# Subtracting two softmaxes on TensorE, with a diagonal of ratios, while the weights are turned: one layer of a streaming encoder on one Trainium2 core

## The chip, the cores and the metric

The kernel runs on one core of a Trainium2 chip. The metric is the device time of one execution in microseconds. Before the change three runs gave 3885.79, 3887.19 and 3892.57 us, median 3887.19 us. The engines are TensorE (PE in the profile, its weight loads PEld), VectorE (DVE), ScalarE (ACT), GpSimd (POOL) and SyncE (SP), and 16 DMA engines move data.

## What is computed

A layer is applied to a prompt of 1024 rows and to 32 rows of a running stream that has 1024 past rows. Everything is float32. The part around the change is differential attention, 8 heads:

```python
s = jnp.einsum('bqhcd,bkhcd->bhcqk', q, k).astype(jnp.float32) * (HEAD_DIM ** -0.5)
visible = k_pos[None, :] < (q_pos[:, None] // CHUNK + 1) * CHUNK
s = jnp.where(visible, s, -jnp.inf)
p = jax.nn.softmax(s, axis=-1)
a = p[:, :, 0] - lam * p[:, :, 1]
return jnp.einsum('bhqk,bkhe->bqhe', a.astype(v.dtype), v)
# then, per head: o = rmsnorm(o, subln_g) * (1 - lam_init)
```

Beside it stand the projections (`z = xn @ w_in`), a short gated convolution, the merge of both branches with sigmoid gates and `w_o`, and a retrieval layer (PEER): each row scores 2 x 128 sub-keys in each of 8 heads, picks 16 of 16384 experts per head, and sums 128 expert rows weighted by a gate and a GELU of a dot product. The cast, norms and the caches are as usual.

## The kernel before

The 1056 rows are nine tiles: tiles 0 to 7 of 128 rows, tile 8 of the 32 stream rows. They are handled in three blocks of three tiles each (`BLOCKS`, L46): tiles 0-2, 3-5, 6-8. Each block has an attention part (`attend`) and then a part of dense products (`middle`). Since the experts of a tile are known only when its block's `middle` is over, the gather of experts of one block runs beside the attention and products of the next.

The backbone is a loop over 1056 slots `q`: one slot is one expert for each of a tile's 128 rows. GpSimd gathers 128 expert rows of 8 KB (L737) into one of nine ring buffers; VectorE forms the 128 dot products (`dot`, L1669); ScalarE applies GELU and the gate (L1256, L1260) and writes a diagonal of the weights (L1267); TensorE adds the weighted rows into PSUM with that diagonal (`weigh`, L1037). 226 of the 1056 slots are added by VectorE (L1680) in place of TensorE. A ring buffer is free for another gather when its row has been added.

Everything else is laid between slots by number: each engine's program yields "due at slot x", and `advance` issues it when the loop reaches that slot (`step_at`, with a pace of 0.93 or less slots per position and seven positions per tile and head, L50-L55). No engine reorders that list, so each runs its instructions in the written order and waits at semaphores.

For one head and one tile (a unit) `attend` does this: scores of both components (L791, mask L795) on TensorE, two row maxima on VectorE (L1477), two exponentials with their sums on ScalarE (L1101) into `pr[:, 0]` and `pr[:, 1]`, then `difference` on VectorE. With unnormalised weights e1, e2 and sums Z1, Z2 it forms `rl = -lambda * Z1 / Z2` (L1483, L1485, one number per row) and `pr0 = e1 + rl * e2` over all keys (L1488); the common factor 1/Z1 is taken up by the norm behind it. `turn_weights` then transposes `pr0` in blocks of 128 keys (L831) into PSUM bank 7, in two halves where there are more than four blocks; ScalarE copies them to SBUF (L1114), and `weigh_values` multiplies them with the values (L850). A unit of tile t has (t+1) key blocks: 4, 5, 6 in the second block of rows and 7, 8 in the third; tile 8 has 8 blocks of 128 keys and one of 32, all with 32 rows. So over 8 heads the second block turns 8 x 15 = 120 key blocks, the third 8 x 15 = 120 of full width and 72 of 32 rows. The exponentials of the next unit wait for `at_d`, that is until this unit's weights are turned.

In the rows below, names stand for buffers: `tl_ps` is PSUM, `tl_u` the scratch space that holds `pr`, `ident` the identity, `tl_dg` the diagonals of the slots, `ringx` and `mix` the ring buffers, `low` the weights' buffers and `tl_xr` normed rows or earlier keys and values.

Of the kernel before, what the change touches and what calls it, by code (L numbers as in the profile page):

```python
# [8 lines left out]
ALU = mybir.AluOpType  # L9
# [4 lines left out]
P = 128  # L14
# [52 lines left out]
def rows_of(t):  # L67

    return DEC if isinstance(t, int) and t == NT else P
# [14 lines left out]
def parts(tensor, first, n, width):  # L84

    return tensor[:, first:first + n * width].rearrange("p (n w) -> p n w", n=n)
# [164 lines left out]
def key_count(t):  # L251

    return (t + 1) * P if t < NT else PAST + DEC
# [7 lines left out]
def turned(w):  # L261

    return sum(turns(BLOCKS[x // 24][2][x % 3]) for x in range(w))


def half_of(b):

    return slice(b * P // 2, (b + 1) * P // 2)
# [23 lines left out]
def build_tail(nc, A, keep):  # L292

    with ExitStack() as ctx:
        def sb(name, shape, dt=F32):
            return ctx.enter_context(nc.sbuf_tensor("tl_" + name, shape, dt))
# [19 lines left out]
        pr = parts(u1, 0, 2, 1056)  # L316
# [16 lines left out]
        rope = sb("rope", [P, 3, 4, HD])  # L333
        ss4, rr4 = sb("ss4", [P, 2, 4]), sb("rr4", [P, 2, 4])
        nb, Z = sb("nb", [P, 2, 2]), sb("Z", [P, 2, 2])
        rl, zz = sb("rl", [P, 1]), sb("zz", [P, 2])
        so, ro = sb("so", [P, 2]), sb("ro", [P, 2])
        early, late = sb("early", [P, P]), sb("late", [P, CHUNK])
        xnr, cvT, oT = xr[:, 0], xr[:, 1], xr[:, 2]
# [48 lines left out]
        ident, ut = keep["ident"], keep["ut"]  # L388
# [363 lines left out]
        def _(pe):  # L752
# [16 lines left out]
            def attend(rb):  # L769
# [49 lines left out]
                def turn_weights(g, i, first, last_block):  # L819
                    t, w = tiles[i], 3 * g + i  # L820
                    n, nk = rows_of(t), key_count(tiles[i])
                    if first == 0:
                        pe.wait_ge(s["df_d"], w + 1)
                        if w:
                            pe.wait_ge(s["op_d"], w)
                    else:
                        pe.wait_ge(s["at_c"], turned(w) + 1)
                    for k in range(first, last_block):
                        m = min(P, nk - k * P)
                        o = ps[:m, 7, k * DEC:(k + 1) * DEC] if t == NT else ps[:, 7, k % 4 * P:(k % 4 + 1) * P]  # L830
                        last = nc.tensor.transpose(o, pr[:n, 0, k * P:k * P + m], ident[:n, :n])  # L831
                    last.then_inc(s["at_d"], 1)

                def weigh_values(g, i):
# [57 lines left out]
                for u in range(-3, 3 * DC + 1):  # L892
# [27 lines left out]
                    if here:  # L920
                        blocks = (key_count(t) + P - 1) // P
                        yield step_at(rb, h, base + TW)
                        turn_weights(g, i, 0, blocks if turns(t) == 1 else 4)
                        if turns(t) == 2:
                            yield step_at(rb, h, base + TW2)
                            turn_weights(g, i, 4, blocks)
# [138 lines left out]
            for b in range(2):  # L1065
                for h in range(2):
                    last = nc.tensor.matmul(ps[:DEC, 2 + h, :], sel[half_of(h), :], xb[half_of(h), 1, b * 512:(b + 1) * 512],
                                            start=b == 0, stop=b == 1)
# [245 lines left out]
        def _(dve):  # L1314
# [154 lines left out]
            def attend(rb):  # L1469
# [9 lines left out]
                def difference(g, i):  # L1479
                    t, w = tiles[i], 3 * g + i  # L1480
                    n, nk = rows_of(t), key_count(t)
                    dve.wait_ge(s["ex_d"], 2 * w + 2)
                    nc.vector.reciprocal(rl[:n, :], Z[:n, w % 2, 1:2])  # L1483
                    dve.drain()
                    nc.vector.scalar_tensor_tensor(out=rl[:n, :], in0=rl[:n, :], scalar=keep["neglam"][:n, 0:1],  # L1485
                                                   in1=Z[:n, w % 2, 0:1], op0=ALU.mult, op1=ALU.mult)
                    dve.drain()
                    nc.vector.scalar_tensor_tensor(out=pr[:n, 0, 0:nk], in0=pr[:n, 1, 0:nk], scalar=rl[:n, 0:1],  # L1488
                                                   in1=pr[:n, 0, 0:nk], op0=ALU.mult, op1=ALU.add).then_inc(s["df_d"], 1)

# [69 lines left out]
                for u in range(-3, 3 * DC + 1):  # L1560
# [12 lines left out]
                    if here:  # L1573
                        if t == NT:
                            yield step_at(rb, h, base + MX1)
                            row_max(g, i, (1,))
                        yield step_at(rb, h, base + (DF1 if t == NT else DF))
                        difference(g, i)
# [128 lines left out]
def build(nc, A):  # L1707
    with ExitStack() as ctx:
        def sb(name, shape, dt=F32):
            return ctx.enter_context(nc.sbuf_tensor(name, shape, dt))  # L1710

        keep = {"ut": sb("ut", [P, DC, 2]), "ident": sb("ident", [P, P]), "mhalf": sb("mhalf", [P, 8]),
                "mix": sb("mix", [P, DC * ROWS]), "ringx": sb("ringx", [P, (RING - 4) * 2 * D]), "low": sb("low", [P, WRING * D]),
                "subg": sb("subg", [P, VD]), "neglam": sb("neglam", [P, 1])}
        keep["xnT"] = parts(keep["mix"], 0, DC, 3 * P)
        keep["gain1"] = keep["mix"][:, DC * ROWS - 3 * D:DC * ROWS - 2 * D]
        keep["tab"] = keep["ringx"][:, 0:(NT + 1) * 4 * HD].rearrange("p (t k d) -> p t k d", k=4, d=HD)
        build_norm1(nc, A, keep)
        build_tail(nc, A, keep)
# [79 lines left out]
```

## Time and profile before

| | |
|---|---|
| median of three runs | 3887.19 us |
| profiled execution, device time | 3888.07 us |
| profiled execution, span | 3886.3 us |
| attention of the second block, about | 780 to 1190 us (24 units) |
| products of the second block | 1190 to 1750 us |
| attention of the third block, about | 1850 to 2385 us (24 units) |
| TensorE busy in the span | 82%, granted clock 0.875 |
| VectorE busy in the span | 65% |

The span is what lies between the first and last recorded instruction; the device time is 1.8 us more. Busy time of an engine in a stretch is the union of its recorded instructions, with a matmul's latency in it. A float32 matmul leaves two records, each with its weight load; a transpose leaves one. The granted clock is 1.00 at 2.4 GHz and 0.50 at 1.2 GHz; a mean between them tells how much of a stretch was spent at either.

### The profile page before, as it was taken

What the parts mean: (1) busy time and instruction counts of PE and PEld (TensorE: products, weight loads), DVE (VectorE), ACT (ScalarE), POOL (GpSimd) and SP (SyncE); (2) the same over time, 40 slices, a digit from 0 to 9 for tenths busy, and PEclk for the clock granted to TensorE, in tenths of its full rate; (3) what the DMA queues carried; (4) which work ended last, traced back from release to release, by engine and by line L of the source; (5) the groups of instructions that cost most, each with busy time, mean ns of one, the idle gap of its engine ahead of it and who ended that gap; (6) DMA issues with size and microseconds to landing.
All of it is one profiled execution on the core that took longest, in us unless ns stands there. A gap on an engine that the chain in (4) does not pass through costs nothing.

```text
span 3886.3 us, 46444 instructions
## 1 busy us (share of the span) xinstructions
PE 3170.0 (82%) x14521; PEld 1452.2 (37%) x14521; DVE 2520.5 (65%) x5855; ACT 1457.8 (38%) x4432; POOL 1498.6 (39%) x1410
## 2 busy tenths in 40 slices
PE   6999997888987999798788787878879667666666
PEld 3555554434443554353333333545335111111111
DVE  3333005988888964777777786886578754556664
ACT  2222002256754244222556565234333333333333
POOL 2111002355654432424455554434354433344442
PEclk9999998889998999898899998988889766666676
DMA  4322336799999999998899999999999999999998
GB/s 161 99 90 78 118 103 233 314 369 365 417 397 396 412 417 394 398 365 323 330 350 388 360 368 412 417 416 417 400 418 417 393 420 420 420 420 419 410 420 335
DMA packets 252964, 1340.70 MB, mean 345 GB/s; under 512 B 27344, under 2 KB 66032, under 8 KB 117296
## 3 DMA queue, kind: packets, MB, share of 16 engines
q0 software_dynamic: 152400, 1108.54, 70.5%
q1 hardware_dynamic: 95472, 215.95, 15.3%
q10 hardware_dynamic: 4848, 13.24, 0.9%
q8 instruction: 117, 1.92, 0.2%
q14 instruction: 127, 1.04, 0.1%
HBM read 1310.49 MB, written 27.15 MB: 344 GB/s over the span
## 4 chain that ended last, share of the span: by engine, by line
PE 46%; DMA 25%; DVE 14%; ACT 8%; issue 3%; DVEq 2%; POOL 1%; ACTq 1%; SPq 0%; POOLq 0%
DMA mix<-in_peer_uv,tl_idx 14%; PE tl_ps L1037 9%; PE tl_ps L983 9%; DMA ringx<-in_peer_uv,tl_idx 8%; PE tl_ps L816 7%; PE tl_ps L1020 4%; PE tl_ps L964 4%; PE tl_ps L996 3%; PE tl_ps L881 3%; DVE mix L1669 2%; PE tl_ps L791 2%; DVE ringx L1669 2%; PE tl_ps L850 2%; DMA mix<-in_peer_uv,tl_itop 1%; DVE tl_xa L1680 1%
## 5 line engine op out<-in xcount | busy, mean ns | idle before, releaser
L737 POOL DMA_INDIRECT ringx<-in_peer_uv,tl_idx x568 | 671.1, 1182 | 919.2 <-PE tl_ps L1037 624.2
L1669 DVE CUSTOM_DVE_ANT_0 ringx<-ringx,tl_xb 128x1024 f32<-128x1024 f32 x585 | 708.6, 1221 | 304.5 <-DMA ringx<-in_peer_uv,tl_idx 273.3
L1037 PE MATMUL tl_ps<-ringx,tl_dg 64*64 64x512 f32 x3808 | 649.5, 769 | 295.8 <-ACT tl_dg L1267 281.4
L737 POOL DMA_INDIRECT mix<-in_peer_uv,tl_idx x456 | 542.7, 1190 | 786.0 <-PE tl_ps L1037 460.7
L1256 ACT ACTIVATE tl_hg<-tl_hd 128x1 f32<-128x1 f32 x1056 | 213.3, 202 | 1436.5 <-DVE tl_hd L1669 1423.0
L1669 DVE CUSTOM_DVE_ANT_0 mix<-mix,tl_xb 128x1024 f32<-128x1024 f32 x471 | 571.5, 1221 | 244.0 <-DMA mix<-in_peer_uv,tl_idx 217.7
L1037 PE MATMUL tl_ps<-mix,tl_dg 64*64 64x512 f32 x2832 | 481.0, 761 | 225.2 <-ACT tl_dg L1267 223.4
L983 PE MATMUL tl_ps<-tl_xr,low 128*128 128x384 f32 (+1 forms) x1280 | 402.5, 471 | 5.0 <-DVE tl_xr L1627 5.0
L1037 PEld LDWEIGHTS tl_ps<-ringx,tl_dg 64*64 64x64 f32 x3808 | 120.6, 155 | 681.3 <-ACT tl_dg L1267 569.9
L1260 ACT ACTIVATE tl_hw<-tl_hg,tl_gw 128x1 f32<-128x1 f32 x1024 | 301.5, 294 | 72.8 <-issue 3.3
L983 PEld LDWEIGHTS tl_ps<-tl_xr,low 128*128 128x128 f32 x1280 | 248.0, 197 | 175.1 <-issue 44.1
L1267 ACT ACTIVATE tl_dg<-tl_eye,tl_hw 128x64 f32<-128x64 f32 x830 | 288.7, 348 | 59.8 <-issue 2.6
L816 PE MATMUL tl_ps<-low,tl_xr 128*128 128x384 f32 (+1 forms) x768 | 297.7, 535 | 15.7 <-DMA low<-in_watt 12.5
L1037 PEld LDWEIGHTS tl_ps<-mix,tl_dg 64*64 64x64 f32 x2832 | 86.9, 154 | 520.3 <-ACT tl_dg L1267 455.3
L1020 PE MATMUL tl_ps<-tl_xr,low 128*128 128x384 f32 (+1 forms) x768 | 263.7, 483 | 1.2 <-ACTq L1228 1.2
L964 PE MATMUL tl_ps<-tl_xr,low 128*128 128x384 f32 (+1 forms) x768 | 236.3, 466 | 0.6 <-ACT tl_xr L1127 0.6
L816 PEld LDWEIGHTS tl_ps<-low,tl_xr 128*128 128x128 f32 (+1 forms) x768 | 137.1, 189 | 191.5 <-issue 104.2
L1020 PEld LDWEIGHTS tl_ps<-tl_xr,low 128*128 128x128 f32 x768 | 140.3, 195 | 135.0 <-issue 75.5
L964 PEld LDWEIGHTS tl_ps<-tl_xr,low 128*128 128x128 f32 x768 | 149.3, 198 | 98.9 <-issue 31.9
L1477 DVE TENSOR_REDUCE tl_nb<-tl_ps 128x1 f32<-128x128 f32 (+5 forms) x144 | 110.6, 805 | 81.4 <-PE tl_ps L795 51.5
L1680 DVE SCALAR_TENSOR_TENSOR tl_xa<-mix,tl_hw,tl_xa 128x1024 f32<-128x1024 f32 x117 | 149.8, 1281 | 5.1 <-issue 4.7
L1634 DVE TENSOR_TENSOR tl_u<-tl_ps,tl_u 128x384 f32<-128x384 f32 (+1 forms) x48 | 25.0, 521 | 191.5 <-PE tl_ps L983 187.2
(205 smaller groups left out, 3878.5 us busy)
## 6 DMA issues: line engine op xcount, KB each, us to landing
low<-in_wall SPq DMA_DIRECT2D x240, 512.0 KB, 7.8
low<-in_watt SPq DMA_DIRECT2D x60, 512.0 KB, 8.3
ringx<-in_peer_uv,tl_idx POOLq DMA_INDIRECT x568, 14.9
mix<-in_peer_uv,tl_idx POOLq DMA_INDIRECT x456, 14.4
ringx<-in_watt SPq DMA_DIRECT2D x12, 512.0 KB, 6.8
tl_u<-in_x_prompt SPq DMA_DIRECT2D x8, 512.0 KB, 11.2
x_rows<-tl_u SPq DMA_DIRECT2D x8, 512.0 KB, 8.1
xs_rows<-tl_u SPq DMA_DIRECT2D x8, 512.0 KB, 8.1
```

Of the source, the lines that this page charges most:

```text
L737: nc.gpsimd.indirect_dma_start(out=ring[q % RING].rearrange("p a d -> p (a d)"), out_offset=None, in_=A["peer_uv"], in_offset=bass.Indirec ...
L816: last = nc.tensor.matmul(o, xn[:, c, i * P:i * P + n], w[:, :, c, :], start=(c == 0), stop=(c == DC - 1))
L881: last = nc.tensor.matmul(ps[:, (3, 5, 3)[k], 0:nr], w[:, c, :], xn[:, c, 0:nr], start=(c == 0), stop=(c == DC - 1))
L964: last = nc.tensor.matmul(ps[:, 2 + 3 * (cc % 2) + k, 0:n], w[:, c, :], xnr[:, c, 0:n], start=(c == 0), stop=(c == DC - 1))
L983: last = nc.tensor.matmul(ps[:, 2 + k, 0:n], w[:, c, :], src[k][:, c, 0:n], start=(c == 0), stop=(c == DC - 1))
L1020: last = nc.tensor.matmul(ps[:, 2 + qb % 2, 0:n], w[:, c, :], xT[:, c, 0:n], start=(c == 0), stop=(c == DC - 1))
L1037: last = nc.tensor.matmul(ps[half_of(h), b, :], dg[rows, npe(q) % DIAGS, :], ring[q % RING][rows, 1, h * 512:(h + 1) * 512], start=k == 0, ...
L1256: nc.scalar.activation(hg[:, j:j + 1], hd[:, j:j + 1], ACT.Gelu)
L1260: gate = nc.scalar.activation(hw[:, j:j + 1], hg[:, j:j + 1], ACT.Copy, scale=table(gw, tops, t)[:, k:k + 1])
L1267: nc.scalar.activation(dg[:, npe(q) % DIAGS, :], eye[:], ACT.Copy, scale=hw[:, j:j + 1]).then_inc(s["dg_done"], 1)
L1669: nc.vector.tensor_tensor_reduce(out=ring[q % RING][:, 0, :], in0=ring[q % RING][:, 0, :], in1=xb[:, t % 2, :], scale=1.0, scalar=0.0, op0 ...
L1680: nc.vector.scalar_tensor_tensor(out=xa[:], in0=ring[q % RING][:, 1, :], scalar=hw[:, k % TOPK:k % TOPK + 1], in1=xa[:], op0=ALU.mult, op1 ...
```

## The change

For the second and third block `difference` no longer touches the weights. VectorE multiplies the 128 x 128 identity by `rl` (one number per row) and so makes a diagonal matrix `ratio`. TensorE then makes each turned block as a sum of two matmuls in PSUM: e1-block times identity plus e2-block times `ratio`. In both, the weights that are loaded are the block of `pr`, and identity or ratio is what streams past. The first block keeps its subtraction and its transposes.

```diff
-        rl, zz = sb("rl", [P, 1]), sb("zz", [P, 2])
+        rl, zz, ratio = sb("rl", [P, 1]), sb("zz", [P, 2]), sb("ratio", [P, P])
...
                     for k in range(first, last_block):
                         m = min(P, nk - k * P)
                         o = ps[:m, 7, k * DEC:(k + 1) * DEC] if t == NT else ps[:, 7, k % 4 * P:(k % 4 + 1) * P]
-                        last = nc.tensor.transpose(o, pr[:n, 0, k * P:k * P + m], ident[:n, :n])
+                        if rb == 0:
+                            last = nc.tensor.transpose(o, pr[:n, 0, k * P:k * P + m], ident[:n, :n])
+                            continue
+                        nc.tensor.matmul(o, pr[:n, 0, k * P:k * P + m], ident[:n, :n], start=True, stop=False, skip_group_check=True)
+                        last = nc.tensor.matmul(o, pr[:n, 1, k * P:k * P + m], ratio[:n, :n], start=False, stop=True, skip_group_check=True)
                     last.then_inc(s["at_d"], 1)
...
                     dve.drain()
+                    if rb:
+                        nc.vector.tensor_scalar(ratio[:n, 0:n], ident[:n, 0:n], rl[:n, 0:1], None, ALU.mult).then_inc(s["df_d"], 1)
+                        return
                     nc.vector.scalar_tensor_tensor(out=pr[:n, 0, 0:nk], in0=pr[:n, 1, 0:nk], scalar=rl[:n, 0:1],
                                                    in1=pr[:n, 0, 0:nk], op0=ALU.mult, op1=ALU.add).then_inc(s["df_d"], 1)
```

Due slots, semaphores and their counts are unchanged. Below, TensorE's order at the first unit of the second block (tile 3, four key blocks), before:

```order
L816 MATMUL tl_ps<-low,tl_xr 128x384 x2
L1037 MATMUL tl_ps<-ringx,tl_dg 64x512 x4
L831 MATMUL tl_ps<-ident,tl_u 128x128 x4
L1037 MATMUL tl_ps<-mix,tl_dg 64x512 x4
L791 MATMUL tl_ps<-tl_xr,tl_u 128x384 x2
```

The same place with the change (line numbers behind L831 are higher by four, L1037 is L1041; `tl_ratio` is the diagonal of ratios):

```order
L816 MATMUL tl_ps<-low,tl_xr 128x384 x2
L1041 MATMUL tl_ps<-ringx,tl_dg 64x512 x4
L834 MATMUL tl_ps<-ident,tl_u 128x128
L835 MATMUL tl_ps<-tl_ratio,tl_u 128x128
L834 MATMUL tl_ps<-ident,tl_u 128x128
L835 MATMUL tl_ps<-tl_ratio,tl_u 128x128
L834 MATMUL tl_ps<-ident,tl_u 128x128
L835 MATMUL tl_ps<-tl_ratio,tl_u 128x128
L834 MATMUL tl_ps<-ident,tl_u 128x128
L835 MATMUL tl_ps<-tl_ratio,tl_u 128x128
L1041 MATMUL tl_ps<-mix,tl_dg 64x512 x4
L791 MATMUL tl_ps<-tl_xr,tl_u 128x384 x2
```

Nothing moved against its neighbours: four transposes became eight matmuls at the same place, ahead of a slot's weighted addition and of the next unit's scores. VectorE's order in a unit of tile 4 (L1669 is the dot product of a slot, L1507 the rotation of the next head's projection), before:

```order
L1483 RECIPROCAL tl_rl<-tl_Z 128x1
L1485 SCALAR_TENSOR_TENSOR tl_rl<-tl_rl,neglam,tl_Z 128x1
L1488 SCALAR_TENSOR_TENSOR tl_u<-tl_u,tl_rl 128x640
L1669 ISA ringx,tl_hd<-ringx,tl_xb 128x1024
L1669 ISA tl_hd 128x1
```

And with the change (seven lines further down in the file, from L1494 on):

```order
L1487 RECIPROCAL tl_rl<-tl_Z 128x1
L1489 SCALAR_TENSOR_TENSOR tl_rl<-tl_rl,neglam,tl_Z 128x1
L1493 TENSOR_SCALAR tl_ratio<-ident,tl_rl 128x128
L1676 ISA ringx,tl_hd<-ringx,tl_xb 128x1024
L1676 ISA tl_hd 128x1
```

One operation over 640 columns became one over 128, with the dot product of a slot queued right behind it as before.

## Rows read from the trace of the kernel before

**Rows 1.** The page: span, busy time by engine, slices of 97 us.

```profile
span 3886.3 us, 46444 instructions
PE 3170.0 (82%) x14521; PEld 1452.2 (37%) x14521; DVE 2520.5 (65%) x5855; ACT 1457.8 (38%) x4432; POOL 1498.6 (39%) x1410
PE   6999997888987999798788787878879667666666
PEclk9999998889998999898899998988889766666676
```

**Rows 2.** Windows by stage: busy us (x instructions), clock, DMA share, GB/s.

```profile
780.00:1190.00 410.00, 352.69 (x2013) 170.71 (x2015) 343.54 (x758) 253.92 (x745) 243.13 (x224) 0.94 0.97 388
1190.00:1750.00 560.00, 523.97 (x2029) 264.33 (x2026) 407.71 (x867) 187.85 (x523) 214.81 (x175) 0.96 0.99 396
1850.00:2385.00 535.00, 435.60 (x2410) 188.05 (x2410) 398.89 (x776) 310.88 (x847) 275.47 (x249) 0.91 0.94 364
3000.00:3886.00 886.00, 580.71 (x2872) 112.66 (x2868) 528.09 (x1127) 312.26 (x1065) 347.20 (x338) 0.68 0.99 407
```

**Rows 3.** Chain of waits, shares by line: second block, then third block.

```profile
by line: PE tl_ps L816 15.2%; PE tl_ps L1037 13.5%; DVE ringx L1669 5.1%; issue 4.7%; PE tl_ps L850 3.7%; DVE mix L1669 3.7%; ACT tl_u L1101 3.6%; ACT L1256 3.4%; PE tl_ps L791 3.4%; ACT L1101 2.8%; ACT tl_hw L1260 2.2%; DVE tl_oh L1388 2.0
by line: PE tl_ps L816 13.0%; PE tl_ps L1037 12.4%; PE tl_ps L791 10.7%; PE tl_ps L850 6.7%; ACT tl_u L1101 6.4%; DMA low<-in_watt 5.2%; issue 5.1%; ACT L1101 4.8%; ACT L1256 4.6%; ACT tl_hw L1260 3.1%; ACT tl_dg L1267 2.2%; PE tl_ps L831 1
```

**Rows 4.** Turns, and last the weighing: xcount | busy us, mean ns | idle.

```profile
L831 PE MATMUL tl_ps<-ident,tl_u 128*128 128x128 f32 x120 | 24.0, 313 | 13.1 <-ACT tl_u L1114 7.4 <-DVE tl_u L1488 5.7
L831 PE MATMUL tl_ps<-ident,tl_u 128*128 128x128 f32 x120 | 21.6, 304 | 9.1 <-ACT tl_u L1114 7.5 <-DVE tl_u L1488 1.6
L831 PE MATMUL tl_ps<-ident,tl_u 32*128 32x32 f32 x64 | 5.4, 224 | 1.8 <-DVE tl_u L1488 1.8
L850 PE MATMUL tl_ps<-tl_u 128*128 128x128 f32 x96 | 14.6, 275 | 0.0
```

**Rows 5.** Timeline of TensorE: start us, us, line, shapes, xrecords.

```profile
1051.63 0.66 PE L831 MATMUL tl_ps<-ident,tl_u 128*128 128x128 f32 x4
1056.74 0.83 PE L850 MATMUL tl_ps<-tl_u 128*128 128x128 f32 x6
...
1153.41 0.44 PE L795 MATMUL tl_ps<-tl_late,tl_early 64*128 64x64 f32 x4
1157.90 1.99 PE L1037 MATMUL tl_ps<-ringx,tl_dg 64*64 64x512 f32 x8 [4.04 <-ACT tl_dg L1267]
1171.23 1.11 PE L831 MATMUL tl_ps<-ident,tl_u 128*128 128x128 f32 x4
...
1927.08 0.71 PE L831 MATMUL tl_ps<-ident,tl_u 32*128 32x32 f32 x9
```

**Rows 6.** Subtraction and nearest small operation on VectorE: mean ns of one.

```profile
L1488 DVE SCALAR_TENSOR_TENSOR tl_u<-tl_u,tl_rl 128x512 f32<-128x512 f32 (+2 forms) x24 | 21.3, 888 | 1.8
L1488 DVE SCALAR_TENSOR_TENSOR tl_u<-tl_u,tl_rl 128x896 f32<-128x896 f32 (+2 forms) x24 | 29.9, 1247 | 1.8
L1488 DVE SCALAR_TENSOR_TENSOR tl_u<-tl_u,tl_rl 32x1056 f32<-32x1056 f32 x8 | 10.4, 1306 | 0.6
L1540 DVE TENSOR_SCALAR tl_u<-tl_u,tl_ro 128x128 f32<-128x128 f32 x16 | 4.6, 289 | 1.5
L1485 DVE SCALAR_TENSOR_TENSOR tl_rl<-tl_rl,neglam,tl_Z 32x1 f32<-32x1 f32 x8 | 1.7, 215 | 0.6
```

**Rows 7.** Windows within the second block: three heads, then two.

```profile
977.97:1114.02 136.05, 130.64 (x790) 64.57 (x791) 113.69 (x246) 95.03 (x285) 92.29 (x84) 1.00 1.02 417
1114.02:1202.54 88.52, 61.76 (x374) 28.54 (x370) 69.80 (x142) 49.90 (x147) 43.30 (x42) 0.86 0.97 382
```

**Rows 8.** Waits of the third block: us, times, longest us.

```profile
POOL ringx L737 <- PE tl_ps L1037: 109.6, 35, 13.1
ACT tl_hg L1256 <- DVE tl_hd L1669: 49.4, 35, 5.1
PE tl_ps L831 <- DVE tl_u L1488: 3.4, 3, 1.6
```

## The prediction

> **What bounds the kernel now.** I read the page first, then the same figures by stage, then the chain of waits in the two stages that the change touches, and last the turns themselves. On the page TensorE is busiest at 82%, but its row of tenths falls to 6 and 7 in the last third, which is another kind of stage [rows 1]. By stage: in the second block's attention (780 to 1190 us) TensorE is busy 352.69 of 410 us and VectorE 343.54, so both stand near 85%; in the third's (1850 to 2385 us) it is 435.60 and 398.89 of 535 us, or 81% and 75%. The dense products between them keep TensorE at 94%. After 3000 us the DMA engines are at 0.99 and 407 GB/s, and both compute engines have a third of their time free [rows 2]. So the touched stages are bound by a chain through several engines. Slots are bound to their places in the program: a stage that takes longer shifts all behind it, and the last stage, which gathers as fast as DMA goes for its own slots, cannot catch up, since a ring of nine buffers holds no more than nine slots ahead.
>
> The chain gives the weights. Of the second block's 410 us it spends 15.2 + 13.5 + 3.7 + 3.4 = 36% in the four TensorE lines that the row shows, and in the three VectorE lines 5.1 + 3.7 + 2.0 = 11% (small lines are cut off). Of the third block's 535 us it is 13.0 + 12.4 + 10.7 + 6.7 = 43% for TensorE, and no VectorE line is among the twelve largest [rows 3]. VectorE is well loaded in the third block, yet the chain seldom passes through it.
>
> Within the second block the state differs by head. Over three heads (nine units, 136.05 us) TensorE is busy 130.64 us, 96%, at a clock of 1.00; over the next five units (88.52 us) it is busy only 61.76 us at 0.86, while VectorE is busy 69.80 us there with expert selection beside the attention [rows 7]. The first kind is bound by TensorE, the second waits for VectorE and ScalarE.
>
> **TensorE's part of the change.** A transposed block of 128 x 128 is one record; four of them take 0.66 us from first start to last end, a record's own duration being 0.31 in the mean, so starts lie about 0.12 us apart. A float32 matmul of 128 x 128 with a 128-column weight load, the form that replaces it, stands in the weighing: two records each, six in 0.83 us with 0.275 us for one, so (0.83 - 0.275) / 5 = 0.111 us per record [rows 4, 5]. A block now needs two matmuls, four records, where one record stood: 3 x 0.111 = 0.333 us more. The second block turns 120 blocks: 40.0 us. The third turns 120 of full width, again 40.0 us, and 72 of the 32-row tile. For those, nine transposes take 0.71 us and one 0.224, so 0.061 us per record; the nearest matmul with a 128-column load and few moving columns (64) does four records in 0.44 us, from 0.05 to 0.08 us each. I take 0.061: 72 x 3 x 0.061 = 13.2 us; at the full 0.111 it would be 24.0. TensorE gets 93.2 us more in all, bounds 90 to 104, and where its clock is at the half the pass costs about double (four transposes 1.11 us there against 0.66) [rows 5]; with means of 0.94 and 0.91 [rows 2], 12% and 18% of the time is at 0.50, which adds up to 15 us.
>
> The Trainium skill, Perfetto Trace Analysis, section Transposes, says that a logical transpose should be a transpose and not a standard matmul, because the transpose path skips the arithmetic. It names no price, and it speaks against this change. Were a matmul as cheap as a transpose, one record, the addition would be 192 + 120 times one record, some 31 us, and by the shares used below the sum would end near +7 us; by the rule, and by the rows' three records more, it ends where this text puts it. The trace agrees with the rule, with 0.22 us for a matmul against 0.12 for a transpose.
>
> **VectorE's part.** Removed are 24 subtractions of 888 ns in the second block, 21.3 us, and 24 of 1247 ns in the third, 29.9 us. Each becomes one operation that scales the identity by one number per row. The same operation and shape is in the norm of the output: 289 ns; for the 32-row diagonal, which is 32 x 32, I take 0.25 us, between a 32 x 1 operation of 215 ns and the 289 [rows 6]. So 24 x 0.289 = 6.9 us and 16 x 0.289 + 8 x 0.25 = 6.6 us come in; VectorE saves 14.4 and 23.3 us, 37.7 in all. ScalarE, GpSimd and the DMA queues get nothing more or less. No wait is added: the first turn still waits for `df_d`, and this signal comes 0.6 us earlier in the second block and 1.0 us earlier in the third. That gain is small where TensorE waits for it: its matmuls stood idle for the subtraction 5.7 us in the second block and 3.4 us in the third [rows 4, 8].
>
> **What of it is on the path.** Second block: in the nine units at 96% I count all of it, 9 x 5 blocks x 0.333 = 15.0 us, and nothing for VectorE. In the other 15 units TensorE has 52 of the stage's 57 us of idle time against 25 us of additional work. Behind each turn stand a slot's weighted addition, the next scores and the projection, so part of it is seen; I take a third, 8 us, and give VectorE's relief of 9 us in those units back by half, 4 us. Sum +19 us. Third block: additional 53.2 us against 99 us of idle time. I take TensorE's share of the chain with something for the cut-off lines, 0.45, so 24 us; VectorE's 23.3 us count at about a sixth, 4 us, for it is nearly absent from the chain [rows 3]. Sum +20 us. Also its GpSimd waits mostly for TensorE to free a ring buffer, 109.6 us on one of the two rings, while ScalarE waits for VectorE's dot products 49.4 us [rows 8]: later turns are late buffers.
>
> Together +39 us on the profiled execution's own 3888.1 us (span 3886.3 and 1.8 around it): 3927. The runs' median is 0.9 us below the profiled execution, so 3926 us.
>
> **Rivals.** (1) Faster: the work hides and VectorE decides. The idle time of TensorE, 57 and 99 us, is larger than 93 us, and most of it in the second block is time in which it waits for a diagonal that hangs on a dot product. If outside the nine full units TensorE's work is wholly covered and VectorE's relief counts in full there (37.7 less 5.4, 32 us), the sum is 15 - 32 = -17: 3870 us. It decides from the point where TensorE's share on the path is under 0.40 (37.7 / 93.2) of VectorE's. For it: VectorE's 84% in the second block. Against it: the chain's weights, 43% against next to nothing in the third block. (2) TensorE binds everywhere. A turn stands in a series: exponential, turn, copy, second turn, copy, weighing, all through one PSUM bank, and the next unit's exponential waits for it. If all of the third block's 53 us and the 25 us of the other units of the second count, with the 15, it is +93 less 18 for VectorE: 3962 us; with half clock as high as 3980. For it: TensorE's idle time before a turn is mostly the wait for ScalarE's copy of the half before (7.4 of 13.1 us, 7.5 of 9.1) [rows 4]. Against it: the units in which TensorE is 70% busy [rows 7]. (3) The clock comes back and it is no change. Half-clock time is about 2 x 0.06 x 410 = 49 us and 2 x 0.09 x 535 = 96 us [rows 2]; if TensorE, with more matmuls between its waits and a VectorE that answers sooner, stayed at full clock, up to half of that, 73 us, would be saved on it, at the weights above (about a half) 36 us: 3890 us. The drop follows an idle wait in the trace: after 4.04 us of waiting for a diagonal eight records take 1.99 us [rows 5]. The turns in the full heads ran at 1.00 with transposes as they are [rows 7], so I hold this small.
>
> **Chances and range.** Forecast case (3905 to 3950) 0.61; rival 1 0.13; rival 2 0.15; rival 3 0.11. Less than 0.2%, some 8 us, can't be told from no change here. Faster: rival 1 and a little of 3, 0.14. Same: most of rival 3 and the edge of the forecast, 0.12. Slower: the forecast and rival 2, 0.74. The range takes in half of rival 3 and rival 2's milder value: 3882 to 3964; the forecast's own range is 3905 to 3950.
>
> **What would show it.** In the changed profile the two new matmul lines have 1248 records at 0.11 us from start to start (0.06 in the 32-row tile), the new VectorE line 48 operations near 0.29 us, and the subtraction only 24, all in the first block. TensorE's busy time rises by 80 to 100 us, VectorE's falls by about 38. The second block's attention is longer by about 19 us, the third's by about 20, the stages before, between and behind within 5 us of what they were. In the three full heads a unit takes 16.8 us in place of 15.1. I am wrong in the pace if a record takes other than 0.11 us; wrong in the path if the stages don't lengthen though TensorE's busy time rose (rival 1), or lengthen by most of the 93 us (rival 2); and rival 3 is shown by granted clocks of 0.97 or more in both stages.

## The result, and the profile after

Four runs of the changed kernel have a median of 3955.09 us (3954.38 to 3956.77) against 3886.9 us for the kernel before: ratio 1.0176, 95% interval 1.0163 to 1.0189. The change makes the kernel 68 us slower. 39 us were forecast, so the result lies just above the forecast's own range (3905 to 3950 us) and inside the wide one (3882 to 3964). The profiled execution took 3954.38 us, with a span of 3952.6 us.

The page after: span, busy time by engine and two rows of slices (99 us each). They answer to [rows 1].

```profile
span 3952.6 us, 48316 instructions
PE 3287.7 (83%) x15457; PEld 1576.3 (40%) x15457; DVE 2484.7 (63%) x5855; ACT 1458.7 (37%) x4432; POOL 1484.0 (38%) x1410
PE   6999998799988999797889988888779767766666
PEclk8999999899998999898899998898889866676666
```

TensorE is busy 117.7 us more (3287.7 against 3170.0) and VectorE 35.8 us less (2484.7 against 2520.5); the forecast was 93 and 38, and 80 to 100 for TensorE was the range named as a sign. By stage, in the columns of [rows 2], with windows moved by the lag:

```profile
780.00:1210.00 430.00, 391.55 (x2367) 216.34 (x2367) 329.56 (x756) 253.91 (x745) 231.69 (x223) 0.95 0.95 371
1210.00:1770.00 560.00, 524.97 (x2035) 266.52 (x2033) 405.90 (x863) 187.56 (x522) 218.39 (x174) 0.96 0.99 394
1870.00:2455.00 585.00, 517.00 (x2986) 266.53 (x2978) 379.87 (x784) 311.69 (x847) 260.66 (x249) 0.89 0.89 336
3070.00:3952.00 882.00, 577.29 (x2852) 109.97 (x2848) 525.66 (x1119) 310.72 (x1059) 350.77 (x337) 0.69 0.99 407
```

The second block's attention takes 20 us more (410 to 430) with TensorE busy 38.9 us more. The third's takes 585 us. The kernel before needs 540 for the same slots, since the window of 535 us in [rows 2] ends one slot or two early; in 1850 to 2390 us its TensorE is busy 439.37 us. So the third block gets 77.6 us more on TensorE and is 45 us longer; TensorE's idle time in it shrank from 100.6 to 68.0 us. The products between and the stage of gathers behind keep their lengths within a few microseconds. The start of each slot's dot product shows the same: the changed kernel is 21 us late behind the second block's attention (slot 340), 67 behind the third's (slot 600), and still 66 at slot 1040. Nothing is given back.

The chain of waits in the second and in the third block, as in [rows 3]:

```profile
by line: PE tl_ps L816 17.3%; PE tl_ps L1041 16.7%; PE tl_ps L834 5.8%; PE tl_ps L791 5.2%; PE tl_ps L854 5.1%; PE tl_ps L835 4.6%; issue 3.4%; ACT tl_u L1105 3.3%; ACT L1260 3.3%; DVE ringx L1676 3.0%; DVE mix L1676 2.7%; ACT L1105 2.7%; D
by line: PE tl_ps L1041 17.9%; PE tl_ps L816 13.4%; PE tl_ps L791 13.2%; PE tl_ps L834 8.4%; PE tl_ps L854 7.1%; PE tl_ps L835 7.0%; ACT tl_u L1105 5.5%; ACT L1105 4.2%; issue 3.3%; ACT L1260 2.9%; ACT tl_hw L1264 1.7%; ACT tl_dg L1271 1.2%
```

In the third block the TensorE lines shown went from 43% to 17.9 + 13.4 + 13.2 + 8.4 + 7.1 + 7.0 = 67% of a longer stretch; the two new lines, L834 and L835, hold 15% of 585 us, 90 us. In the second they hold 10.4% of 430 us, 45 us.

The new operations in the third block (form, x records, busy us, mean ns), against [rows 4, 6]:

```profile
L834 PE MATMUL tl_ps<-ident,tl_u 128*128 128x128 f32 x240 | 52.2, 301 | 5.5 <-ACT tl_u L1118 4.8 <-DVE tl_ratio L1493 0.6
L834 PE MATMUL tl_ps<-ident,tl_u 32*128 32x32 f32 x128 | 25.6, 280 | 0.5 <-DVE tl_ratio L1493 0.5
L835 PEld LDWEIGHTS tl_ps<-tl_ratio,tl_u 32*128 32x128 f32 x128 | 20.2, 197 | 0.0
L1493 DVE TENSOR_SCALAR tl_ratio<-ident,tl_rl 128x128 f32<-128x128 f32 x16 | 4.9, 304 | 1.2
L1493 DVE TENSOR_SCALAR tl_ratio<-ident,tl_rl 32x32 f32<-32x32 f32 x8 | 2.1, 262 | 0.6
```

The diagonal's price came out as estimated: 304 and 262 ns against 289 and 250. The full-width record too. The 32-row tile did not. One of its turns, timeline of TensorE (L834 and L835 alternate, two records each):

```profile
2025.10 0.40 PE L834 MATMUL tl_ps<-ident,tl_u 32*128 32x32 f32 x2
2025.35 0.38 PE L835 MATMUL tl_ps<-tl_ratio,tl_u 32*128 32x32 f32 x2
2025.57 0.38 PE L834 MATMUL tl_ps<-ident,tl_u 32*128 32x32 f32 x2
...
2028.47 0.38 PE L835 MATMUL tl_ps<-tl_ratio,tl_u 32*128 32x32 f32 x2
2028.79 0.24 PE L834 MATMUL tl_ps<-ident,tl_u 32*32 32x32 f32 x2
2028.87 0.22 PE L835 MATMUL tl_ps<-tl_ratio,tl_u 32*32 32x32 f32 x2
2029.02 2.73 PE L1041 MATMUL tl_ps<-ringx,tl_dg 64*64 64x512 f32 x12
```

From 2025.10 to 2029.02 us are 3.9 us for 36 records, of which the 32 with a 128-column load start 0.11 us apart (2025.35 to 2025.57 is two), and the last four, with a load of 32 columns, about 0.04 (2028.79 to 2028.87 is two). [rows 5] has 0.71 us for the nine transposes. I had taken 0.061 us per record.

Behind this turn the eight-record group of a slot and the first half of the next stand as one row of 2.73 us for 12 records. That is slow: the eight records ahead of this turn took 1.09 us. The windows of the turn and of what follows it tell why (the column after the five engines is the granted clock):

```profile
2025.10:2028.90 3.80, 3.80 (x39) 3.76 (x36) 3.54 (x15) 1.77 (x4) 0.94 (x1) 1.00 0.86 327
2029.20:2032.50 3.30, 3.30 (x16) 0.56 (x12) 1.26 (x3) 1.85 (x8) 1.16 (x3) 0.50 0.40 156
```

The clock goes from 1.00 to 0.50 although TensorE was busy all of the 3.8 us ahead. In the third block of the kernel before (1850 to 2385 us) the clock fell 17 times, each time with idle time of TensorE in the last few microseconds before it.

### The profile page after: what moved, and what is told of

Same layout as the page of the kernel before. It is cut to its first block, busy times and chain, and to the rows that moved or that the text cites. A ratio compares the mean times of both kernels' runs of the same rounds, so it can differ in the third digit from the quotient of the medians.

```text
span 3952.6 us, 48316 instructions
## 1 busy us (share of the span) xinstructions
PE 3287.7 (83%) x15457; PEld 1576.3 (40%) x15457; DVE 2484.7 (63%) x5855; ACT 1458.7 (37%) x4432; POOL 1484.0 (38%) x1410
## 4 chain that ended last, share of the span: by engine, by line
PE 51%; DMA 23%; DVE 13%; ACT 7%; issue 3%; DVEq 1%; POOL 1%; ACTq 1%; SPq 0%; POOLq 0%
DMA mix<-in_peer_uv,tl_idx 13%; PE tl_ps L1041 10%; PE tl_ps L987 9%; DMA ringx<-in_peer_uv,tl_idx 9%; PE tl_ps L816 8%; PE tl_ps L1024 4%; PE tl_ps L968 4%; PE tl_ps L1000 3%; PE tl_ps L885 3%; PE tl_ps L791 3%; PE tl_ps L854 2%; DVE ringx L1676 2%; DVE mix L1676 2%; PE tl_ps L834 2%; PE tl_ps L835 2%
## 5 line engine op out<-in xcount | busy, mean ns | idle before, releaser
L1041 PE MATMUL tl_ps<-ringx,tl_dg 64*64 64x512 f32 x3808 | 648.7, 767 | 279.9 <-ACT tl_dg L1271 265.5
L737 POOL DMA_INDIRECT mix<-in_peer_uv,tl_idx x456 | 552.4, 1211 | 825.7 <-PE tl_ps L1041 502.0
L1041 PE MATMUL tl_ps<-mix,tl_dg 64*64 64x512 f32 x2832 | 477.2, 756 | 213.2 <-ACT tl_dg L1271 211.5
L1041 PEld LDWEIGHTS tl_ps<-ringx,tl_dg 64*64 64x64 f32 x3808 | 119.9, 155 | 661.1 <-ACT tl_dg L1271 552.1
L1041 PEld LDWEIGHTS tl_ps<-mix,tl_dg 64*64 64x64 f32 x2832 | 86.7, 153 | 505.6 <-ACT tl_dg L1271 440.4
```

Source lines behind the costliest of these rows:

```text
L737: nc.gpsimd.indirect_dma_start(out=ring[q % RING].rearrange("p a d -> p (a d)"), out_offset=None, in_=A["peer_uv"], in_offset=bass.Indirec ...
L1041: last = nc.tensor.matmul(ps[half_of(h), b, :], dg[rows, npe(q) % DIAGS, :], ring[q % RING][rows, 1, h * 512:(h + 1) * 512], start=k == 0, ...
```

## The experiments

Times are medians; "before" was run beside each. Differences are against it, with the ratio's 95% interval. Two of the kernels leave the second softmax out of the result, "VectorE's relief alone" in the second and third block and "tile 8, first pass only" in tile 8.

| kernel | us | against before | ratio, interval |
|---|---|---|---|
| changed | 3955.1 | +68.2 | 1.0176 (1.0163 to 1.0189) |
| second block alone | 3911.5 | +25.6 | 1.0065 (1.0048 to 1.0082) |
| full width alone, tile 8 as before | 3937.6 | +51.8 | 1.0131 (1.0115 to 1.0148) |
| tile 8 alone | 3918.4 | +32.6 | 1.0083 (1.0066 to 1.0100) |
| tile 8 with all 128 rows | 3956.7 | +70.9 | 1.0184 (1.0167 to 1.0201) |
| VectorE's relief alone | 3881.4 | -5.4 | 0.9987 (0.9978 to 0.9997) |
| TensorE's work alone | 3963.2 | +76.4 | 1.0198 (1.0181 to 1.0215) |
| tile 8, first pass only | 3936.6 | +49.8 | 1.0131 (1.0114 to 1.0148) |
| transpose, then add | 3918.7 | +31.9 | 1.0087 (1.0070 to 1.0103) |
| before, one slot in four on VectorE | 3883.4 | -3.6 | 0.9993 (0.9984 to 1.0002) |
| transpose, then add, one in four | 3902.3 | +15.2 | 1.0041 (1.0026 to 1.0057) |

**Which block, which tile.** Three kernels restore the old way in part of the work, with the same condition in `turn_weights` and in `difference`.

```diff
-                        if rb == 0:
+                        if rb != 1:
...
-                    if rb:
+                    if rb == 1:
```

> The new turning in the second block alone; the third has its subtraction on VectorE and its transposes again. Before is 3887 us, the changed kernel 3955. The slots of the changed trace run 21 us late behind the second block's attention and 67 us behind the third's, so every theory expects 3908 us (3905 to 3911) if the two blocks' losses add up; over 3915 or under 3900 would mean that they don't, and that the slots' lag is not how to divide the loss.

3911.5 us, 25.6 us over before and half a microsecond over the interval stated, where the forecast for this block was 19. What is left for the third block is 43 us, where 20 were forecast. So the surprise is in the third block.

```diff
-                        if rb == 0:
+                        if rb == 0 or t == NT:
...
-                    if rb:
+                    if rb and t != NT:
```

> The 32-row tile has its subtraction on VectorE and its transposes again, the full-width tiles 3 to 7 keep the new turning. Theory A (the third block loses more than forecast because of the 32-row tile: its turn takes 3.75 us in place of 0.68, 8 times, and TensorE's clock is at the half right behind 7 of the 8 turns): 3955 less 25 less 5 to 15 for the clock, 3915 to 3925 us, and no half-clock stretch that begins inside a busy turn. Theory B (the third block is a series through TensorE, in which the full-width turns, 40 us, count whole, as rival 2 of the prediction had it): the 32-row tile is worth its forecast 13 us or less, 3942 us or more.

3937.6 us, between both theories: tile 8 is worth 17.5 us of the changed kernel, less than A said and more than B.

```diff
-                        if rb == 0:
+                        if t != NT:
...
-                    if rb:
+                    if t == NT:
```

> The counterpart: only the 32-row tile has the new turning, tiles 0 to 7 are as before. Theory A: 25 us of longer turns and 5 to 15 us of half clock, less 1 us a turn that VectorE no longer subtracts, 3912 to 3925 us. Theory B: 3895 to 3902 us. If this loss and that of the kernel with tile 8 transposed add up to the 68 us, the tiles' losses are independent.

3918.4 us, 32.6 over before: in A's range. But the two don't add up: 51.8 + 32.6 = 84 us, where both together lose 68. Part of the missing 16 us is a wait that the kernel before happens to have. Third block, waits on the load of a head's projection weights (us, times, longest), before first, with three others that are used below; then with tile 8 alone:

```profile
PE tl_ps L816 <- DMA low<-in_watt: 12.5, 1, 12.5
PE tl_ps L1037 <- ACT tl_dg L1267: 51.1, 38, 5.2
ACT tl_u L1114 <- PE tl_ps L831: 8.8, 5, 3.5
PE tl_ps L791 <- ACT tl_u L1101: 24.2, 8, 4.6
```

```profile
PE tl_ps L816 <- DMA low<-in_watt: 8.5, 1, 8.5
```

The weights of a head land late once, and TensorE waits 12.5 us for them. In the changed kernel this wait is 0.2 us, as its rows below show, and with full width alone it is 11.6. Here added work in TensorE took the place of idle time, and only when both parts are there does most of it vanish. That covers 12 us less 4.0 and 0.9 that the single parts had saved already, some 7 of the 16; the rest stays open.

```profile
ACT tl_u L1118 <- PE tl_ps L835: 34.0, 24, 5.2
PE tl_ps L1041 <- ACT tl_dg L1271: 37.5, 25, 5.2
ACT tl_hg L1260 <- DVE tl_hd L1676: 32.3, 23, 4.1
ACT tl_u L1114 <- PE tl_ps L835: 19.1, 8, 3.7
PE tl_ps L816 <- DMA low<-in_watt: 0.2, 1, 0.2
PE tl_ps L791 <- ACT tl_u L1105: 24.2, 8, 4.6
```

These are waits of the changed kernel's third block. The copies of turned blocks (L1114 and L1118, L1110 and L1114 before) now wait for TensorE 34.0 + 19.1 us (8.8 + 0.7 before), while TensorE's own wait for a diagonal of a slot went from 51.1 to 37.5 us only.

**Is it the clock?** The turn of tile 8 loads and streams all 128 rows.

```diff
-                        nc.tensor.matmul(o, pr[:n, 0, k * P:k * P + m], ident[:n, :n], start=True, stop=False, skip_group_check=True)
-                        last = nc.tensor.matmul(o, pr[:n, 1, k * P:k * P + m], ratio[:n, :n], start=False, stop=True, skip_group_check=True)
+                        nc.tensor.matmul(o, pr[:, 0, k * P:k * P + m], ident[:, :n], start=True, stop=False, skip_group_check=True)
+                        last = nc.tensor.matmul(o, pr[:, 1, k * P:k * P + m], ratio[:, :n], start=False, stop=True, skip_group_check=True)
```

> The changed kernel, but the 32-row tile's turn loads all 128 rows of the weights' buffer and streams 32 columns of all 128 rows of the identity and of the ratios. Rows 32 to 127 of those columns are zeros, so the sums are the same, and the count and shape of the records' columns too. It asks what the clock's fall inside these turns hangs on. If it is that only 32 rows of the array work, the stretches at half clock that begin inside a turn vanish, a turn stays at 0.11 us per record (about 4 us), and the time falls by the 5 to 15 us that theory A puts to the clock, to 3940 to 3950 us. If it is the 32 columns, or the clock costs nothing here, it stays at 3955 within 3 us. A load that depended on the rows would show as another pace than 0.11 us.

The third block of this kernel, same columns as above:

```profile
1870.00:2455.00 585.00, 509.63 (x2986) 263.75 (x2986) 379.87 (x785) 311.98 (x847) 259.30 (x249) 0.91 0.89 335
```

The mean clock rose from 0.89 to 0.91, and TensorE was busy 509.63 us in place of 517.00. The time did not fall: 3956.7 us, where theory A expected 3940 to 3950. So the clock's 5 to 15 us do not show. That they are nothing isn't shown, though. At the 0.67 us per microsecond that is measured below, 7.4 us of busy time would be worth 5 us (an estimate), the four runs of this kernel spread over 5 us (3955.2 to 3960.2), and the wait for the same late weights, 0.2 us in the changed kernel, was back at

```profile
PE tl_ps L816 <- DMA low<-in_watt: 4.5, 1, 4.5
```

which may have taken back what the clock gave. The clock still fell in or right behind four of the eight turns, against seven, so what it hangs on isn't settled either.

**Two halves of the change.** VectorE's relief alone keeps the transposes of the first softmax and leaves out the second; TensorE's work alone keeps the subtraction, and the second matmul has a diagonal of zeros.

```diff
-                        if rb == 0:
+                        if True:
```

> VectorE's part alone: in the second and third block VectorE makes the diagonal and doesn't subtract, and TensorE transposes the first softmax's weights as before. The second softmax is left out of the result. TensorE's instructions are those of the kernel before (3886 us in these runs). Theory C (the relief counts little, as the forecast's 4 and 4 us): 3876 to 3882 us. Theory D (the relief of 38 us counts for a good part, and the changed kernel's 68 us are what is left after it): 3850 to 3868 us, and TensorE's part would be 90 us or more.

```diff
+            nc.gpsimd.memset(ratio[:], 0.0)
...
-                    if rb:
-                        nc.vector.tensor_scalar(ratio[:n, 0:n], ident[:n, 0:n], rl[:n, 0:1], None, ALU.mult).then_inc(s["df_d"], 1)
-                        return
```

> TensorE's part alone: VectorE subtracts as before, and TensorE turns with the two matmuls, the second with a diagonal of zeros, which changes no sum. The counterpart of the kernel with VectorE's relief alone. Theory C: 3955 plus 4 to 12 us, 3959 to 3967. Theory D: 3973 to 3993. If TensorE's and VectorE's parts add up, this and the other one together are 68 us from before.

Busy times of the whole span, relief alone first and TensorE's work alone second:

```profile
PE 3167.8 (82%) x14521; PEld 1448.4 (37%) x14521; DVE 2483.3 (64%) x5855; ACT 1457.9 (38%) x4432; POOL 1496.5 (39%) x1410
```

```profile
PE 3283.9 (83%) x15457; PEld 1576.1 (40%) x15457; DVE 2522.6 (64%) x5855; ACT 1459.0 (37%) x4432; POOL 1484.6 (37%) x1411
```

VectorE is busy 37.2 us less in the first, and that is worth 5.4 us. TensorE is busy 113.9 us more in the second, and that costs 76.4. The sum is +71, the whole change +68: the halves add up within the intervals, and theory C holds. (Beside TensorE's added work the relief is worth 8 us, 3963.2 less 3955.1.) A microsecond taken from VectorE here is worth about 0.15 us (5.4 / 37.2; the interval of the 5.4 us is 1 to 9), one given to TensorE costs 0.67 (76.4 / 113.9).

**What a matmul is worth, at its place.** Tile 8 without its second matmul, so that the second softmax is missing there, and then every first pass as a transpose to which the second adds:

```diff
-                        nc.tensor.matmul(o, pr[:n, 0, k * P:k * P + m], ident[:n, :n], start=True, stop=False, skip_group_check=True)
+                        last = nc.tensor.matmul(o, pr[:n, 0, k * P:k * P + m], ident[:n, :n], start=True, stop=t == NT, skip_group_check=True)
+                        if t == NT:
+                            continue
```

> The changed kernel, but in the 32-row tile the second matmul of a block is left out (the second softmax is missing there): 18 records in place of 36 a turn. At 0.11 us a record, that the 128-column load sets, a turn takes about 2.0 in place of 3.75 us: 14 to 16 us less on TensorE. If all of a tile-8 turn is on the path (theory B for this tile), 3939 to 3942 us; by the forecast's share of 0.45, 3948 us; if the clock's fall counts too (theory A), 3930 to 3937, since shorter turns don't reach it.

```profile
PE 3261.3 (83%) x15313; PEld 1555.5 (40%) x15313; DVE 2484.3 (63%) x5855; ACT 1458.9 (37%) x4432; POOL 1482.9 (38%) x1410
```

3936.6 us, 18.5 us less, for about 16 us less of turning and 26.4 us less of busy time. By the records alone the share is about 1, by busy time 0.70 (18.5 / 26.4), and not 0.45 by either; the runs lie apart (3930.6 to 3938.8), and more can't be read from it. The time lies at the edge of theory A's range (3930 to 3937), below theory B's (3939 to 3942). The clock fell in or right behind three of these eight turns, against seven, so this run does not clear the clock either.

```diff
-                        nc.tensor.matmul(o, pr[:n, 0, k * P:k * P + m], ident[:n, :n], start=True, stop=False, skip_group_check=True)
+                        nc.tensor.transpose(o, pr[:n, 0, k * P:k * P + m], ident[:n, :n])
```

> The changed kernel, but the first pass of each block is a transpose (one record) and the second, with the ratios, a matmul that adds to it in PSUM: three records in place of four. The sum is the same if PSUM adds to what a transpose has written. TensorE gets less: 240 x 0.11 and 72 x (0.22 - 0.06), some 38 us. By the forecast's share of 0.45 that is 17 us, 3938; by the share of about 0.7 that the third block shows (43 of some 65 us), 27 us, 3928 us. If a change between transposing and multiplying costs something each time, 312 times 2, it is nearer to 3955 or above; 0.1 us each would eat all of it.

The first two blocks and the fourth of a four-block turn of this kernel, and its busy times:

```profile
906.57 0.33 PE L834 MATMUL tl_ps<-ident,tl_u 128*128 128x128 f32 x1
906.73 0.39 PE L835 MATMUL tl_ps<-tl_ratio,tl_u 128*128 128x128 f32 x2
906.95 0.27 PE L834 MATMUL tl_ps<-ident,tl_u 128*128 128x128 f32 x1
907.06 0.39 PE L835 MATMUL tl_ps<-tl_ratio,tl_u 128*128 128x128 f32 x2
...
907.73 0.39 PE L835 MATMUL tl_ps<-tl_ratio,tl_u 128*128 128x128 f32 x2
908.04 1.09 PE L1041 MATMUL tl_ps<-ringx,tl_dg 64*64 64x512 f32 x8
```

```profile
PE 3231.6 (82%) x15145; PEld 1523.2 (39%) x15145; DVE 2485.0 (63%) x5855; ACT 1459.5 (37%) x4432; POOL 1483.3 (38%) x1410
```

A block now takes three records, and the switch between the two kinds costs nothing inside the turn: 906.73 to 906.95 us is two records of a matmul, 906.95 to 907.06 one of a transpose. TensorE is busy 56.1 us less than in the changed kernel, and the time falls by 36.4 us to 3918.7, more than half of the change's loss. Both forecasts, 3938 and 3928, were too high: they counted 38 us of records, where busy time fell by 56.1, of which 36.4 is a share of 0.65. It is the best way to do this on TensorE of those tried, and still 32 us slower than before. The Trainium skill (Perfetto Trace Analysis, Transposes) asks for a transpose where one is meant, and not a matmul: these 36 us are what following that rule for the first pass gives back.

**The exchange the other way.** The kernel before, with 12 slots of the third block's attention moved from TensorE to VectorE:

```diff
-SHARED = ((0,170,1,6),(170,300,3,4),(336,520,1,6),(520,680,2,3))
+SHARED = ((0,170,1,6),(170,300,3,4),(336,520,1,4),(520,680,2,3))
```

> The kernel before, with one number changed: beside the third block's attention (slots 336 to 520) VectorE adds one slot's rows in four and no longer one in six, 38 slots in place of 26. It moves 12 x 1.02 us from TensorE to VectorE, where one costs 1.28 us: the opposite exchange to the change's. Theory C' (a microsecond on TensorE is worth about 0.8 in these stages and one on VectorE about 0.14, as the two halves of the change measured alone show, 76 us for TensorE's and -5 us for VectorE's): 12.2 x 0.8 - 15.4 x 0.14, 8 us faster, 3876 to 3882 us where before is 3887. Rival: the weights are no property of the engines but of the turn's place in the series, and a slot moved elsewhere is worth nothing or costs, since the ring buffer that VectorE adds from comes free later: 3886 to 3892 us.

3883.4 us, 3.6 less; the interval holds 1. The sign is the expected one and the size, 8, is not: the time lies between both ranges, 3876 to 3882 and 3886 to 3892, and whether it is faster at all stays open. The prices of 0.8 and 0.14 give about twice the measured gain here. The same edit and `(0,170,1,4)` on top of the kernel that transposes and then adds:

> The kernel that transposes and then adds (3919 us), with VectorE adding one slot in four and no longer one in six beside the attention of the second block, and of the third (24 slots more, 12 in each; the first slots of the second block's stage come ahead of its attention): VectorE's relief of 38 us is spent on taking work from TensorE. Theory C': 24 x 1.02 x 0.8 = 20 us off, and 24 x 1.28 x 0.14 = 4 us on: 3900 to 3906 us, still slower than before, because the relief of 38 us buys 29 slots at most, and these are 30 us of TensorE's time against some 50 that the added matmuls cost. Rival: 3915 to 3925 us.

3902.3 us, as expected (3900 to 3906), 16.4 us less: VectorE's free time can be spent, but it buys less than the turns cost.

## Why the prediction was right in direction and low in size

- **The mechanism** was right: the turn becomes dearer on TensorE than the subtraction was on VectorE, both blocks lose, and nothing comes back in the stage of gathers. The price on the path was not: the measured 3955.1 us is 5 us outside the forecast's own range, and it falls in the wide range because that took in rival 2's milder value.
- **VectorE's part** was right: 37.7 us forecast, 37.2 measured alone, counted at 8 and worth 5.4 (1 to 9).
- **The second block** was nearly right: 19 us forecast, 25.6 measured. The nine full units took 15.0 us each by the starts of their turns, and 16.5 us after (978.42 to 1127.28), where 16.8 was forecast against 15.1. That is 13.8 us for the nine, where 15.0 were forecast, so what is missing is in the other units, where I let TensorE's idle time cover two thirds and expected 4 us net; the trace of the changed kernel, 21 us late in all, leaves 7 for them, and the times of the second block alone leave 12.
- **The price of the 32-row tile** was mis-sized, 13.2 us. With 0.11 us per record a turn went from 0.71 to 3.99 us (first start to last end, six of the eight turns), 26 us over eight heads; the bound of 24.0 stated beside it was near. The row I took for the nearest, the mask's matmuls (0.05 to 0.08 us), also loads 128 columns, but they belong to two matmuls on different halves of the array's rows. Singly their four records start at 1153.42, 1153.47, 1153.53 and 1153.58 us: if they alternate between the halves, each half has one per 0.11 us. That this is why the row looked faster was not tried.
- **TensorE's share in the third block, 0.45, was the step that failed**, and the amount that it was applied to was too small. 53.2 us were counted as 24, and with VectorE's 4 us the block at +20. Measured, 77.6 us of busy time make it 45 us longer, with VectorE's relief in it. Of the 24 us of additional busy time some 13 are the 32-row tile; the rest goes with the lower clock (a mean of 0.89 against 0.91), for which the prediction named up to 15 us and took none into its sum. At a share of 0.45 the true amount would give 31 us (an estimate); the other 14 are the share, which is about 0.63 ((45 + 4) / 77.6). The single edits agree with that: 0.67 for TensorE's work alone, 0.70 and 0.65 for the two edits of the turn.
- **Why the share was too low.** The chain of the profile before gave 43% because TensorE's waits for ScalarE and for a DMA stood between its works; I read this share as the chance that more work is on the path. But the turn is followed on TensorE by the next unit's scores, on which the row maximum, the exponential and the next turn hang. My reading, which no run takes apart further, is that work added in such a series is on the path unless the wait that it runs into has another cause. The rows bear it out in part. Ahead of tile 8's scores TensorE waits for an exponential once per head, and this wait did not shrink: 24.2 us in eight waits, before and after. What did shrink were the waits for the slots' diagonals (51.1 to 37.5 us) and the one for the weights' DMA (12.5 to 0.2), 25.9 of the 32.6 us of idle time that the added work filled.
- **The rivals.** Rival 1, that VectorE decides, fell with the relief measured alone. Rival 3, that the clock comes back, fell too: 0.95 and 0.89 against 0.94 and 0.91, where it wanted 0.97 or more. Rival 2, TensorE on the path everywhere (3962 us), is nearer to the result than the forecast (7 us off against 29; the stages of attention lengthen by 65 us, most of the 93 us that were its sign), and its reason, the series through one turn, agrees with what the third block shows.

## What to carry to other kernels

A share of the chain of waits is what an engine's present work weighs; work added to it in the middle of a series can cost well over that (0.67 here against 0.36 and 0.43). Ask of each idle stretch which wait ends it, and whether the added work stands ahead of that wait's cause. Of two engines that are busy 75 to 86% of the same stages, one was worth 0.15 us per microsecond of relief, and the other cost 0.67: measure each half of an exchange alone. If a sum of two matrices must be turned on TensorE, transpose the first and let a matmul add the second.

## What the runs showed of the hardware

- A float32 matmul leaves two records, and with a load of 128 columns each starts 0.11 us after the one before, also where only 32 columns stream; a float32 transpose with the same load and 32 columns takes 0.06, and one with 128 columns 0.11. With a load of 32 columns the matmul's records were about 0.04 us apart. So in these matmuls the pace went with the columns loaded, and not with those streamed.
- A float32 matmul can add in PSUM to what a float32 transpose wrote there, at no loss of time (three records in 0.33 us, 906.73 to 907.06).
- The clock fell from 1.00 to 0.50 within or right behind turns of some 3.8 us in which TensorE was busy without a gap, with loads of 32 rows by 128 columns and 32 columns streamed, in seven of eight such turns, and in four of eight with 128 rows. The mean clock of the stage went from 0.89 to 0.91 between the two, and the time did not fall with it.
